# Two chained transformer blocks on one core: scores that wait per head, l2 sums and decays moved into the projections, and products without a use in idle places

## The reference

```python
def l2norm(x):
    return x * lax.rsqrt(jnp.sum(x * x, axis=-1, keepdims=True) + EPS_2)

# delta rule, layer 0 of block 2
qkv = silu(centred_conv(concat([hq, hk, hv]), conv_w))
q = l2norm(q) * A_DK ** -0.5
k = l2norm(k)
beta = sigmoid(hb)
g = -exp(a_log) * softplus(ha + dt_bias)
...
# windowed attention, layer 0 of block 2, per key head and group of 4 query heads
s = q @ k.T - slope * dist          # masked by distance
p = softmax(concat([s, sink]))
# dense attention, layer 1 of block 2
p = softmax(q @ k.T)
# feed-forward
h = h + square(relu(rmsnorm(h) @ w_ff1)) @ w_ff2
```

## Time and profile before

| | |
|---|---|
| median of 3 runs | 2038.95 us (2037.88 to 2044.79) |
| time of the profiled execution | 2032.38 us |
| its span, first to last instruction | 2030.5 us |
| mean granted TensorE clock | 0.913 of full speed |
| busy: PE / PEld / DVE / ACT | 1729.9 / 1181.4 / 828.6 / 478.5 us |

### The profile page before, as it was taken

How to read it: one execution, slowest core, us unless ns; L and a number is a source line. 1 busy time by engine, 2 the same in 40 slices (tenths; PEclk the granted TensorE clock), 3 DMA queues, 4 the chain that set the end, 5 groups by cost and what they waited for, 6 DMA issues and landing times.

```text
span 2030.5 us, 22320 instructions
## 1 busy us (share of the span) xinstructions
PE 1729.9 (85%) x8993; PEld 1181.4 (58%) x8995; DVE 828.6 (41%) x1734; ACT 478.5 (24%) x863; POOL 0.5 (0%) x7
## 2 busy tenths in 40 slices
PE   7958999998985899999699665876789998778998
PEld 5645444433664444434285454864389994438998
DVE  7772410111315230101362846554345654625655
ACT  1142111101123211111122421110134431423443
POOL 0000000000000000000000000000000000000000
PEclk9958999999996999999899577977899999898999
DMA  8061489999323359999920000002425424202541
GB/s 296 1 227 56 164 330 394 394 396 365 126 105 124 110 169 391 395 396 392 365 102 0 1 1 0 1 1 105 143 101 185 170 83 166 83 0 75 210 171 62
DMA packets 153352, 348.05 MB, mean 171 GB/s; under 512 B 8240, under 2 KB 15280, under 8 KB 153280
## 3 DMA queue, kind: packets, MB, share of 16 engines
q1 hardware_dynamic: 145616, 338.28, 45.3%
q10 hardware_dynamic: 7664, 8.78, 1.3%
HBM read 346.00 MB, written 1.05 MB: 171 GB/s over the span
## 4 chain that ended last, share of the span: by engine, by line
PE 69%; DVE 11%; DMA 11%; ACT 3%; issue 2%; SPq 2%; ACTq 0%; DVEq 0%
PE ps L712 66%; DMA ring<-in_w_up 10%; DVE ring L1766 2%; SPq L622 2%; DVE arena L1766 2%; DMA ring<-in_w_in 1%; DVE ring L1772 1%; PE ps L1040 1%; ACT arena L1565 1%; PE ps L1076 1%; PE ps L719 1%; DVE h L1766 1%; ACT hT L1366 0%; DVE small L2195 0%; DVE small L1934 0%
## 5 line engine op out<-in xcount | busy, mean ns | idle before, releaser
L712 PE MATMUL ps<-ring,arena 128*64 128x512 f32 (+6 forms) x1728 | 387.7, 585 | 28.9 <-DMA ring<-in_w_up 18.5
L712 PE MATMUL ps<-ring,hT 128*128 128x512 f32 (+5 forms) x816 | 331.1, 565 | 11.8 <-ACT hT L1366 7.2
L712 PE MATMUL ps<-arena_r,ring_r 128*128 128x272 f32 (+1 forms) x1024 | 294.5, 288 | 0.0
L712 PEld LDWEIGHTS ps<-ring,arena 128*64 128x64 f32 (+2 forms) x1728 | 140.7, 145 | 258.2 <-issue 251.3
L712 PEld LDWEIGHTS ps<-ring,hT 128*128 128x128 f32 (+1 forms) x816 | 149.1, 185 | 183.3 <-issue 159.2
L1366 ACT ACTIVATE arena<-ps 128x512 f32<-128x512 f32 (+7 forms) x179 | 79.9, 475 | 557.8 <-PE ps L712 353.1
L712 PEld LDWEIGHTS ps<-arena_r,ring_r 128*128 128x128 f32 x1024 | 196.3, 192 | 0.0
L712 PE MATMUL ps<-arena_r,ff_hi_r 128*128 128x272 f32 (+1 forms) x992 | 186.2, 285 | 2.8 <-DVE arena L1766 2.8
L712 PE MATMUL ps<-ring 128*128 128x128 f32 (+2 forms) x848 | 132.8, 324 | 51.4 <-DVE ring L1766 30.3
L712 PE MATMUL ps<-arena_r,y_r 128*128 128x272 f32 (+1 forms) x544 | 152.9, 293 | 26.5 <-DVE ring_r L1766 23.4
L712 PE MATMUL ps<-arena 128*128 128x512 f32 (+8 forms) x418 | 122.6, 493 | 40.2 <-DVE small L1769 25.5
(11 more groups left out here) (281 smaller groups left out, 1590.1 us busy)
## 6 DMA issues: line engine op xcount, KB each, us to landing
ring<-in_w_down SPq DMA_DIRECT2D x32, 2048.0 KB, 14.6
ring<-in_w_gate SPq DMA_DIRECT2D x32, 2048.0 KB, 17.7
ring<-in_w_up SPq DMA_DIRECT2D x32, 2048.0 KB, 19.3
ring<-in_w_ff SPq DMA_DIRECT2D x32, 2048.0 KB, 8.3
ring<-in_w_in SPq DMA_DIRECT2D x8, 2048.0 KB, 19.9
ring<-in_w_in_ab SPq DMA_DIRECT2D x5, 2048.0 KB, 14.3
ring<-in_w_o SPq DMA_DIRECT2D x4, 2048.0 KB, 11.6
ring<-in_ple_gate SPq DMA_DIRECT2D x4, 2048.0 KB, 19.8
```

What stands on the lines that cost most here:

```text
L712: return pe.matmul(o, lhsT, rhs, start=a, stop=z)
```

## The change

There are three edits.

1. **Per-head waits in `attend`** (both layers of block 2). `masked` raises a new semaphore `s_taken` when scores have left PSUM: after each head in layer 0, for all four at once after the copy in layer 1. `score(i+1)` waits for it before each head instead of for `s_ready`.
2. **l2 sums and decays in the projections.** The sums of squares (`head_sums`) stand between the last projection groups, ScalarE takes their logarithm there (`log_sums`), and one exponential over all eight heads with scale -0.5 (`l2_inv`) takes the place of eight roots and eight reciprocals. The decay inputs of VectorE stand before the norms of the window queries, ScalarE's `decay_exps` among the projections. The transposes of the window queries go to banks 4 to 7.
3. **Products with unused results** (`stay_busy`): 128 by 512 products of the identity with constants, written to a free bank. Per layer of block 1, 3 before the second `normed_tile` and 2 after it; 5 at the head of `normed_T` except the first time (three times); 7 before the wait for `mix2_ready`; 6 before the first `hidden` of each feed-forward part, behind the wait for `uT_ev`. These are 44 products in all.

```diff
+            def stay_busy(bank, count):
+
+                for _ in range(count):
+                    mm(ps[:, bank, :], ident, consts[:, 0:512], True, True)
...
+                stay_busy(2, 3)
                 normed_tile(2 * l, 1)
+                stay_busy(7, 2)
                 normed_tile_in(2 * l, 0)
...
             def normed_T(n, hn):
 
+                if n > 0:
+                    stay_busy(7, 5)
...
                 def score(i):
                     t, g = steps[i]
-                    if i > 0:
-
-                        pe.wait_ge(s_ready, base + i)
                     for hd in range(GRP):
+                        if i > 0:
+                            pe.wait_ge(s_taken, GRP * (base - ATT_BASE[0] + i - 1) + hd + 1)
                         ins = mm(ps[0:tile_rows(t), hd, 0:LT], q(t, g, hd), k(g), True, True)
...
+            def head_sums(c):
+
+                pe.wait_ge(sq_ready, c + 1)
+                if c >= 4:
+                    pe.wait_ge(l2_log, c - 3)
+                mm(ps[:, c % 4, 0:LT], ones[:, :], cacc[:, c, :], True, True).then_inc(l2_mm, 1)
...
-            for c in range(2 * A_H):
-                pe.wait_ge(sq_ready, c + 1)
-                if c >= 4:
-                    pe.wait_ge(l2_root, c - 3)
-                mm(ps[:, c % 4, 0:LT], ones[:, :], cacc[:, c, :], True, True).then_inc(l2_mm, 1)
+                if i >= NA + 4:
+                    head_sums(i - NA - 4)
+            for c in range(NAB - NA - 4, 2 * A_H):
+                head_sums(c)
...
+            stay_busy(5, 7)
             pe.wait_ge(mix2_ready, 1)
...
+                stay_busy(7, 6)
                 for q in range(4):
                     hidden(FF_UNITS[L] + q, q, 0, q, 0)
...
+            def decay_exps():
+
+                act.wait_ge(const2_load, 80)
+                act.wait_ge(decay_dve, 1)
+                for t in range(NT2):
+                    r = rows(t)
+                    act.activation(beta3[0:r, t, :], tkvb[0:r, t, 0:8], ACT.Sigmoid)
+                link(act.activation(neg_a, p_alog, ACT.Exp))
+                link(act.activation(edec, sp_t, ACT.Abs))
+                link(act.activation(edec, edec, ACT.Exp, scale=-1.0))
+
+            def log_sums(c):
+
+                act.wait_ge(l2_mm, c + 1)
+                act.activation(cacc[:, c, :], ps[:, c % 4, 0:LT], ACT.Ln, bias=eps2).then_inc(l2_log, 1)
...
+                if c == 1:
+                    decay_exps()
+                if c == 3:
+                    act.activation(edec, edec, ACT.Ln, bias=1.0).then_inc(decay_act, 1)
+                if c >= 3:
+                    log_sums(c - 3)
...
+            act.wait_ge(l2_log, 2 * A_H)
+            act.activation(cacc[:, :, :], cacc[:, :, :], ACT.Exp, scale=-0.5).then_inc(l2_inv, 1)
...
                         for hd in range(GRP):
                             slope = 2.0 ** (-8.0 * (4 * g + hd + 1) / B_H)
-                            ins = stt(probs[i % 3][0:r, hd, :], C(f"neg_dist{t}")[0:r, :], slope, ps[0:r, hd, 0:LT], ALU.mult, ALU.add)
-                        link(ins)
+                            stt(probs[i % 3][0:r, hd, :], C(f"neg_dist{t}")[0:r, :], slope, ps[0:r, hd, 0:LT], ALU.mult, ALU.add).then_inc(s_taken, 1)
+                        dve.wait_ge(s_taken, GRP * (i + 1))
...
-                        link(dve.tensor_copy(probs[i % 3][0:r, :, :], ps[0:r, 0:4, 0:LT]))
+                        dve.tensor_copy(probs[i % 3][0:r, :, :], ps[0:r, 0:4, 0:LT]).then_inc(s_taken, GRP)
+                        dve.wait_ge(s_taken, GRP * (base - ATT_BASE[0] + i + 1))
...
+                dve.wait_ge(l2_inv, 1)
                 for c in range(2 * i, min(2 * i + 2, 2 * A_H)):
-                    dve.wait_ge(l2_root, c + 1)
-                    link(dve.reciprocal(cacc[:, c, :], cacc[:, c, :]))
                     stt(qkvF[:, c, 0:LT], qkvF[:, c, 0:LT], A_D ** -0.5 if c < A_H else 1.0, cacc[:, c, :], ALU.mult, ALU.mult).then_inc(l2_done, 1)
```

More of the change, by code:

```diff
@@ L407, in program @@
         conv_done, conv_act, sq_ready = sem("conv_done"), sem("conv_act"), sem("sq_ready")
-        l2_mm, l2_root, l2_done = sem("l2_mm"), sem("l2_root"), sem("l2_done")
+        l2_mm, l2_log, l2_inv, l2_done = sem("l2_mm"), sem("l2_log"), sem("l2_inv"), sem("l2_done")
+        s_taken = sem("s_taken")
         tok_mm, tok_ev = sem("tok_mm"), sem("tok_ev")
@@ L1636, in _ @@
                     act.activation(cacc[:, c, :], qkvF[:, c, 0:LT], ACT.Square).then_inc(sq_ready, 1)
+                if c == 1:
[4 more added lines that the diff above has]
+                    log_sums(c - 3)
             for c in range(NAB - 2 - NA, 2 * A_H):
                 act.activation(cacc[:, c, :], qkvF[:, c, 0:LT], ACT.Square).then_inc(sq_ready, 1)
-            for c in range(2 * A_H):
-                act.wait_ge(l2_mm, c + 1)
-                act.activation(cacc[:, c, :], ps[:, c % 4, 0:LT], ACT.Sqrt, bias=eps2).then_inc(l2_root, 1)
+            for c in range(NAB - 2 - NA - 3, 2 * A_H):
+                log_sums(c)
             act.wait_ge(qT2_mm, 3)
             for t in range(NT2):
[L1646 to L1662, removed]
+                copy(qpT[:, :, cols(t)], heads(ps[:, 4 + t, :])[:, :, 0:rows(t)]).then_inc(qT2_ev, 1)
+            copy(kpT, ps[:, 7, 0:LT]).then_inc(qT2_ev, 1)
+            act.wait_ge(l2_log, 2 * A_H)
+            act.activation(cacc[:, :, :], cacc[:, :, :], ACT.Exp, scale=-0.5).then_inc(l2_inv, 1)
+            attend(0, w_prob, w_pT, rows)
             for n in range(6):
@@ L2273, in _ @@
                 ins.then_inc(conv_done, 1)
+            dve.wait_ge(ab_ev, 4 * 3 + NT2)
+            dve.wait_ge(const2_load, 80)
+            link(dve.memset(beta_t, 0.0))
+            link(dve.memset(g_t, 0.0))
+            link(dve.memset(sp_t, 0.0))
+            for t in range(NT2):
+                r = rows(t)
+                ins = tt(sp3[0:r, t, :], tkvb[0:r, t, 8:16], p_dt[0:r, :], ALU.add)
+                link(ins)
+            dve.tensor_copy(tB[:, 0:1], sp_t[:, 0:1]).then_inc(decay_dve, 1)
             dve.wait_ge(ab_ev, 4 * 3 + 2 * NT2)
-            dve.wait_ge(const2_load, 80)
             link(ts(gqs[:, 0:B_HD], p_bq, B_HD ** -0.5, None, ALU.mult))
@@ L2290, in delta_inputs @@
             def delta_inputs(i):
-                if i == 0:
-                    link(dve.memset(beta_t, 0.0))
-                    link(dve.memset(g_t, 0.0))
-                    link(dve.memset(sp_t, 0.0))
-                    for t in range(NT2):
-                        r = rows(t)
-                        ins = tt(sp3[0:r, t, :], tkvb[0:r, t, 8:16], p_dt[0:r, :], ALU.add)
-                        link(ins)
-                    dve.tensor_copy(tB[:, 0:1], sp_t[:, 0:1]).then_inc(decay_dve, 1)
+                dve.wait_ge(l2_inv, 1)
                 for c in range(2 * i, min(2 * i + 2, 2 * A_H)):
-                    dve.wait_ge(l2_root, c + 1)
-                    link(dve.reciprocal(cacc[:, c, :], cacc[:, c, :]))
                     stt(qkvF[:, c, 0:LT], qkvF[:, c, 0:LT], A_D ** -0.5 if c < A_H else 1.0, cacc[:, c, :], ALU.mult, ALU.mult).then_inc(l2_done, 1)
@@ L2306, in delta_inputs @@
                     dve.wait_ge(decay_act, 1)
-                    link(stt(tA[:, 0:24], sp_t, 0.0, tA[:, 0:24], ALU.max, ALU.add))
+                    link(stt(edec, sp_t, 0.0, edec, ALU.max, ALU.add))
                     link(ts(neg_a, neg_a, -1.0, None, ALU.mult))
@@ L2310, in delta_inputs @@
                         r = rows(t)
-                        ins = tt(g3[0:r, t, :], tA[0:r, 8 * t:8 * t + 8], neg_a[0:r, :], ALU.mult)
+                        ins = tt(g3[0:r, t, :], edec[0:r, 8 * t:8 * t + 8], neg_a[0:r, :], ALU.mult)
                         link(ins)
```

6 lines of the change are left out of this document (3 added, 3 removed).

## The result

The changed kernel takes 2012.9 us (median of 4 executions, 2011.4 to 2013.9) against 2038.4 (4 executions, 2034.0 to 2044.8): a ratio of 0.9873, 95% interval 0.9855 to 0.9891. The forecast was 2013.

A forecast was written before the change was run, and what follows sets the result against it. With PE busy for 85% of the span, time could only come from PE waiting or running slow. Terms 17 + 4.3 + 2.8 + 0.6 + 3.4 - 2.4 = 25.7 us took 2032.4 to 2006.7; plus 6.6 gave 2013, range 2006 to 2018.

The forecast's parts named there:

- Window attention, 17: Window attention and its head: copies 1.5 us earlier, first mask gap 4.1, later steps shorter; 12.7 to 21.5 gained, 17 taken.
- the tail: End of the window attention: up to 0.8 us gained.
- Dense attention, 4.3: Dense attention: scores start earlier and finish before the shares; 4.3 us gained, bounds 3.0 and 5.5.
- Products in block 1, 2.8: First norm of block 1: products fill PE's waits, router falls from 4.9 to 3.5 us; 1.4 gained a layer, 2.8 us.
- Ahead of `normed_T`, 0.6: Products ahead of the transposes, three times: 0.6 us gained in all, from 0 to 1.5.
- After the scan, 3.4: Seven products before the projection: they start slow, then projection and transposes run faster; 3.4 us gained, bounds 2 and 4.
- Ahead of `hidden`, -2.4: Six products ahead of each feed-forward part's first hidden overshoot a too short place: 2.4 us lost, bounds -5 and +1.5.
- The median: Whole kernel: the median of runs lies 6.6 us above the profiled execution, added to 2006.7 us.
- PE at the low clock: Rival: PE stays at 0.50 through the window attention, gaining 12.7 instead of 17, dense 3.0; 2019 us, chance 0.20.
- The head waits do nothing: Rival: attention steps stay 10.2 us, 1.5 of the attention's gain left and no dense gain; 2033 us, chance 0.04.
- Products slow and holding the queue: Rival: added products run at the low clock and overshoot their places, 32.8 us lost against 21.3; 2050 us, chance 0.04.
- Transposes do not hold the clock: Rival: clock falls over transposes, losing block 1's 2.8 and most of the 3.4 after the scan; 2019 us, chance 0.08.

The follow-up runs named there:

- experiment 12: The changed kernel plus the edits of experiment 8 and experiment 9, and masked tile i waiting for the turn of tile i-3 instead of i-2: 2001.1 us, ratio 0.9822.
- experiment 1: The kernel before with only the per-head waits in both attentions of block 2: 2029.8 us, ratio 0.9960 to the kernel before.
- no_fill: The changed kernel without any of the 44 products with unused results: 2026.6 us, ratio 0.9939 to the kernel before.
- experiment 6: The changed kernel without the ten products around the first norm of block 1, other 34 kept: 2019.4 us, ratio 0.9904 to the kernel before.
- no_fill_hidden: The changed kernel without the twelve products ahead of the first hidden products, other 32 kept: 2010.8 us, ratio 0.9878 to the kernel before.
- experiment 9: The changed kernel with more unused products in the window attention, while query copies run and ahead of each turn's wait: 2010.3 us, ratio 0.9864.
- experiment 7: Same run as no_fill_hidden: the changed kernel without the twelve products ahead of the first hidden products: 2010.8 us, ratio 0.9878 to the kernel before.
- Experiment 8: The changed kernel with four products before and four behind the wait for evicted transposes, instead of six behind it, ahead of hidden: 2005.8 us, ratio 0.9843.
- fill_only: The kernel before with only the 44 products with unused results added: ratio 0.9981 to the kernel before, 5.0 us faster by the medians.
- busy_inverse: The changed kernel with 24 more unused products, eight in each of three idle gaps of the inverse: 2013.9 us, ratio 0.9888 to the kernel before.
- sums_only: The kernel before with only the moved l2 sums, logarithms and decays, no head waits or added products: 2042.3 us, ratio 1.0025.
- experiment 11: The kernel before, unchanged, profiled a second time: 2037.8 us, against 2032.4 us in the first profiled execution.
- experiment 5: The changed kernel with its 44 unused products on 64 rows instead of 128, same columns, count and places: 2033.0 us, ratio 0.9975.

## Why the prediction was right, and where it was not

The total was right to 0.1 us, and that closeness is luck: the sum of 25.7 us put the profiled execution at 2006.7 us, and it took 2012.4, while the 6.6 us added on top of it came out as 0.6. The two errors cancel. The largest term, the window attention, was right by its mechanism.

- **Window attention, 17.** Traces: 1.8 in the projections and 15.0 in the attention, 16.8. By steps: the copies started 1.9 earlier (1.5 forecast), mask 1 stands 3.97 behind mask 0 (3.4 forecast: score(1) at the low clock still makes it wait 0.57), and mask 1 to mask 5 takes 30.2 us, in the forecast 26.0 to 34.0. The sentence that a mask still waits for `turn(i-2)` is what the rows show at every mask from 2 on; experiment 12 removed that wait. Experiments 1 and 2 confirm the main step, that VectorE's reciprocals and PE's scores have to go together. In the tail nothing was gained.
- **Dense attention, 4.3.** 5.8 in the trace, above its bound of 5.5: the scores that were priced at the low clock's 3.63 ran at 2.10, with less idle time ahead of them (1.48 instead of 3.00). That this kept the clock up is not shown: in both traces of before the next scores ran at 2.10 too, after 2.98 us of idleness. In `no_fill`, where a turn and a weighing there ran at 0.50, the part took 38.0 us and 3.6 were gained.
- **Products in block 1, 2.8.** Half of the mechanism held: the router took 3.61 us, and 1.3 and 1.4 us are gained at the two norms against the trace shown. The other half did not, that what PE gains ahead of the weight loads moves them all. From the last products ahead of the first norm to the end of block 1 the change is 0.3 us shorter than that trace, 1.6 shorter than the second one, whose router took 6.34 us and whose norms lost 3.6 and 2.9 us more, and 1.0 shorter than the kernel of experiment 6. So a quarter or less of the gain at the norms was left at the end.
- **Ahead of `normed_T`, 0.6.** No run isolates it. The dense attention behind the second of these places took 38.0 us in `no_fill`, but 35.9 in `heads_only` with no product either, and 38.1 in `no_fill_hidden` with them: the table shows no effect.
- **After the scan, 3.4.** Two values: 1.8 in the change and two others, 3.4 in five. The low clock of 2.4 to 5.8 us that the forecast took behind the start of the products, like the 3.4 to 6.8 us ahead of `hidden`, was read from no row; the runs show 0 and 3.4 us here and 6.8 us there. The forecast had them starting slow and overshooting; in the change they ran at full clock, 6.17 us, ended early, and PE idled 1.77 us. Then the clock fell to 0.50 for 3.4 us and the projection took 43.49 us, not the 41 forecast. In experiment 9 they took 7.43, left 0.55 idle, and the projection took 41.87:

```profile
1381.68 7.43 PE L713 MATMUL ps<-consts 128*128 128x512 f32 x14
1389.66 1.44 PE L1259 MATMUL ps<-consts,ring 128*128 128x128 f32 x12 [0.55 <-DVE small L2442]
1391.83 41.87 PE L713 MATMUL ps<-ring,hT 128*128 128x512 f32 x96 [0.73 <-DVE hT L1793]
```

- **Ahead of `hidden`, -2.4.** In the traces of before and after the two parts are 1.9 and 0.2 us longer, where the forecast had 0.5 and 1.9; experiment 7 gives 2.2 us by the medians, within the error. The reason given, a place shorter than the products, holds. Experiment 8 adds that the clock had fallen in the idle time in front of the wait, and that filling it turns the loss into a gain against no products, 4.9 us by the medians and 3.3 in the two parts of the traces.
- **Not in the sum.** The delta rule took 223.9 to 229.3 us in the twelve changed kernels and 222.7 in both traces of before. Read at the same VectorE instructions, 3.5 to 4.2 us of the surplus stand in the last steps of the scan in seven traces (`heads_only`, `no_fill`, `fill_only`, the change, `no_fill_block1`, `busy_inverse`, `all_three`), and at most 0.1 in the five others. The same scan step on PE, before and in `heads_only`, each with the start of the next:

```profile
1367.90 1.16 PE L712 MATMUL ps<-ring 128*128 128x128 f32 x8 [2.23 <-DVE ring L1766]
1375.82 1.16 PE L712 MATMUL ps<-ring 128*128 128x128 f32 x8 [2.24 <-DVE ring L1766]
```
```profile
1366.87 1.88 PE L713 MATMUL ps<-ring 128*128 128x128 f32 x8 [2.24 <-DVE ring L1766]
1377.64 1.16 PE L713 MATMUL ps<-ring 128*128 128x128 f32 x8 [2.24 <-DVE ring L1766]
```

The step lasts 7.9 us at 1.00 and 10.8 where the clock stood at 0.50 for 6.8 of them; TensorE's wait for VectorE is the same, so the slower products lie on the path. The code of the scan is the same in both, and the forecast had no term for a clock that falls elsewhere. Why it falls where it does remains open. The same goes for the 2.2 us ahead of the dense attention, and for `sums_only`, whose dense attention (45.0 us) and qkv stretch (59.4) are longer at unchanged code, with more stretches at 0.50. Such differences hold most of what the products seem to add to the two other edits.
- **The median.** The 6.6 us by which it stood above the profiled execution were added whole. The change's median came out only 0.6 above its profiled time. So 20.0 us between the profiled times and 5.5 of that slack make the 25.5; experiment 11 puts the slack into slow norms and projections, which the forecast's terms had priced from the luckier trace.

The rivals. *PE at the low clock* was half true: it held for 20.5 us, and the forecast had 7.8 us for the first two steps. Three steps took 7.8 to 7.9; it rose before the third was over, and the step after took 6.6, so that 16.8 us came instead of 12.7. *The head waits do nothing* is refuted by experiment 1 (4.7 us in the window attention, 5.7 in the dense one). *Products slow and holding the queue* is what experiment 5 made true: by the traces 15.8 of its 19.3 us stand after the scan (5.8, with the 4.5 counted in the delta rule) and in the feed-forward parts (10.0), which the rival named. In block 1, which it named too, nothing was lost. *Transposes do not hold the clock* would have lost the gains around the first norm and after the scan; both are there, and the eight transposes between the products took 1.09 us at 1.00. The Trainium skill ("TensorE: Matmul & The Clock Gate", Part 4) says that full clock doesn't engage for transposes; the router behind them ran at 1.00 all the same, but so short a stretch of them, between products, is a weak test. The 24 transposes ahead of the first feed-forward part took 2.56 us at 1.00 in the change, against 4.00 before.

## What to carry to other kernels

When a step has two chains of nearly equal length across two engines, cost them together: removing one shows little, removing both shows the whole. A product without a use paid in this kernel where TensorE was on the chain right behind it, placed before the clock fell, with full rows, and sized to leave neither overshoot nor a gap. Ahead of the weight loads of block 1 most of the gain was lost again, and in the inverse the clock fell a little later instead. And take a second trace of the kernel before, before sizing a term from its clock, and add up the parts in which nothing was changed: here they moved by more than most of the terms.

## What the runs showed of the hardware

- Twelve records on 64 of 128 rows ran for 10.6 us ahead of `hidden`, and fourteen for 12.3 us after the scan, with the clock at 0.50 to the end. On 128 rows the twelve of the change began at 0.50 and ended at 1.00 (8.22 us). After the scan the fourteen of experiment 9 also began at 0.50, were at 1.00 from 1384.2 on, and took 7.43 us; in the change they ran at 1.00 throughout. The scores of the window attention are products on 64 rows as well, and stood at 0.50 while TensorE was busy 18.4 of 20.5 us.
- A scan step with the same instructions and the same waits lasts 7.9 us at 1.00 and 10.8 with 6.8 us at 0.50, though TensorE is busy only 5.0 of the 7.9.
- The same program has different times: 2033.9 to 2045.4 for the kernel before in one set of 17 executions, 2028.1 to 2043.7 for `fill_only` in 12, but 1999.7 to 2002.6 for `all_three` in 5. Two traces of the kernel before differed by 5.5 us in block 1 and the projections, with the clock at 0.50 for 17 us more in these two, and by 0.03 in the 920 us behind.
